# The mixers' output product by Strassen's seven block products, on the machinery of the MLP's down-projection

## The chip, the core and the metric

The kernel runs on one NeuronCore of a Trainium2 chip: TensorE (PE) multiplies matrices into PSUM, VectorE (DVE) and ScalarE (ACT) work elementwise, GpSimd (POOL) masks and loads, SyncE (SP) issues most transfers from HBM. The metric is the device time of one execution in microseconds; of several runs the median is taken.

## The reference, cut to what matters

Two transformer blocks in float32 on 512 tokens of width 1024. The first ends its two mixers (a chunkwise mLSTM, `y_a`, and a stick-breaking attention, `y_b`) with gates and an output product, and goes on with an MLP of width 4096:

```python
gates = jax.nn.sigmoid(jnp.concatenate([g_a, g_b], axis=-1).astype(jnp.float32) + b_gate[l])
y = gates[..., :D_MODEL] * y_a + gates[..., D_MODEL:] * y_b
x = x + y.astype(x.dtype) @ w_out[l]                              # (512 x 1024) @ (1024 x 1024)
h2 = rms_norm(x, norm_mlp_g[l])
x = x + jnp.square(jax.nn.relu(h2 @ w_up[l])) @ w_down[l]
```

The second block (a sparse attention with three branches, gates, an output product and a norm) starts with a norm of this `x`.

## The kernel before

**Products.** Every float32 operand is split into a high part, rounded to fp32r by ScalarE (`split_hi`, L602, for weights), and a fine part, the rest, by VectorE (`split_lo`, L610). A product is three matmuls: high x high, high x fine, fine x high. Weights come in slabs of 1 MB (`slabs`): 1024 rows of 256 columns, or 512 rows of 512 columns ("wide"). A slab is loaded to one of two raw buffers, split into one of two pairs `w_hi`, `w_lo`, and used; a slab's split waits until the slab two before it has been used. Each engine works strictly in the order in which its code is written; semaphores are the only ties between them.

**Gate stage.** Slabs `gb` (4 slabs, 8 tiles of 128 features by 512 tokens, 24 matmuls each, L633) give the second gate. The tiles take turns in the two banks of `ps_g`. For each of them ScalarE applies the sigmoid (L784), VectorE multiplies by `yb_f` (L871) and adds `y_f` (L872), ScalarE casts the sum to `y_hi` (L787), VectorE makes `y_lo` (L875), and only that frees the bank. Before every second tile each of the two engines has a weight split.

**Output product.** Four wide slabs `wo` of `w_out`, 4 token tiles each, 12 matmuls of 128x512 to a tile (`mm_half`, L656). Two tiles go to banks of `ps_z`, two to `ps_g`. VectorE adds each finished tile to `x_sb` (L885).

**Norm and transpose.** `act_rms` squares and sums the four token blocks of x (L944), takes the square root of blocks 0 to 2 and later of block 3 (L948); VectorE takes the reciprocal and scales (`dve_rms`, L958 to L966); TensorE transposes (`feature_tiles`, L684); ScalarE and VectorE write `act_hi`, `act_lo` (L741, L754). This happens ahead of the MLP and again ahead of the second block; the second time its banks become free with the last products (`late`).

**MLP.** Four rounds over quarters of the hidden width. A round has four `up` slabs (8 tiles: relu, square, cast, fine part L880) and then a 512x1024 by 1024x1024 product by Strassen's algorithm in the Winograd form, in seven block products M1, M2, M6, M5, M7, M3, M4, called product 1 to 7 in this order: 256 tokens by 512 by 512, 24 matmuls each (`down_product`, L1277). Its operands need sums of blocks. VectorE makes four sums for each of four feature tiles (`mix_up`, L1890 to L1896) and their fine parts (`mixed_lo`, L1902), and four sums of weight blocks of 128x2048 (`mix_weights`, L1926); ScalarE makes the high parts (L1610). Seven weight splits follow. M1 is copied (L1616), and VectorE adds 14 half products of 128x512 to `x_sb` (L1940). Product 1 needs tiles 0 to 3 of the eight, product 2 tiles 4 to 7.

**Loads.** SP issues all weight loads in one queue: the slabs in order, and the four blocks of `w_down` of a round into `down_raw` (`load_down`), as their buffers come free.

Of the kernel before, what the change touches and what calls it, by code (L numbers as in the profile page):

```python
# [29 lines left out]
P = 128  # L30
# [99 lines left out]
def program(nc, a, out):  # L130

    with ExitStack() as ctx:
# [36 lines left out]
        y_hi = sb("y_hi", [P, KT, S], F32R, at=arena + 3 * K16)  # L169
        y_lo = sb("y_lo", [P, KT, S], F32R, at=arena + 4 * K16)  # L170
# [256 lines left out]
        N_WO = add_wide("wo", a["w_out"], 0, 2)  # L427
        N_MLP = len(slabs)
        for quarter in range(4):
            add("up", a["w_up"], quarter * D, 4)  # L430
            for p in range(PRODUCTS):
                slabs.append((None, quarter, 0, WIDE, "down", p, None))
# [22 lines left out]


# [50 lines left out]
        for n in range(N_ALL):  # L507
            if slabs[n][4] == "down":
                if slabs[n][5] == M7:
                    raw_of[n] = raw_of[n - M7 - 2]  # L510
                    last[raw_of[n]] = n
                continue
# [57 lines left out]
        def raw(n):  # L570

            if slabs[n][4] == "down" and slabs[n][5] != M7:
                return down_raw[DOWN_RAW[slabs[n][5]]]
            return w_raw[raw_of[n]]
# [183 lines left out]
        def act_evacuate(act, n, i):  # L758
# [10 lines left out]
            if kind in ("if", "wo"):  # L769
                return  # L770
# [12 lines left out]
            elif kind == "gb":  # L783
# [3 lines left out]
                nc.scalar.copy(y_hi[:, f, :], ev_t[:, g, :]).then_inc(ev_act, 1)  # L787
# [45 lines left out]
        def dve_evacuate(dve, order, n, i):  # L833
# [175 lines left out]
        def _(sp):  # L1009
# [21 lines left out]
            for n in range(N_MLP):  # L1031
                if n == 1:
                    sp.wait_ge(raw_landed[0], 16)
                load_slab(n)
            down_rows = a["w_down"].rearrange("(q h k p) n -> p q h k n", h=2, k=HALF_K, p=P)

            def load_down(q, i):

                if q == 0:
                    sp.wait_ge(tile_ready, tile_of[N_MLP] - 2)  # L1040
                else:
                    last_split = {0: M6, 1: M4, 2: M5, 3: M3}[i]
                    sp.wait_ge(lo_done, N_MLP + MLP_SLABS * (q - 1) + 4 + last_split + 1)
                    if i == 0:
                        sp.wait_ge(mixed_w, 4 * q)
                src = down_rows[:, q, i % 2, :, WIDE * (i // 2):WIDE * (i // 2 + 1)]
                sp.dma_start(down_raw[i][:], src).then_inc(down_in[i], 16)

            for q in range(4):
                n = N_MLP + MLP_SLABS * q  # L1050
                if q == 0:
                    load_slab(n)
                    load_slab(n + 1)
                    for i in range(4):
                        load_down(q, i)
                else:
                    load_down(q, 0)
                    load_down(q, 2)
                    load_slab(n)
                    load_slab(n + 1)  # L1060
                    load_down(q, 3)
                    load_down(q, 1)
# [24 lines left out]
        def _(pe):  # L1087
# [150 lines left out]
            for n in range(N_WO, N_WO + 4):  # L1238
                mm_slab(pe, n, tile_of[N_GB] if n == N_WO else None, y_hi, y_lo)


            feature_tiles(pe, N_MLP, lambda b: xn[b], lambda b: pe.wait_ge(xn_ready, TB + b + 1),
                          before=N_MLP - 1)
            def down_product(q, p):

                n = N_MLP + MLP_SLABS * q + 4 + p
                up0 = tile_of[n - p - 4]
# [34 lines left out]
            for q in range(4):  # L1282
                n = N_MLP + MLP_SLABS * q
                for j in range(4):
                    mm_slab(pe, n + j, activation_ready=features_ready(pe, N_MLP, 1) if q == j == 0 else None)
                for p in range(PRODUCTS):
                    down_product(q, p)


            def late_banks():  # L1290
                pe.wait_ge(prod_added, added(3, M4, 1))

            pe.wait_ge(prod_added, added(3, M3, 1))
            feature_tiles(pe, N_NQ, lambda b: xn[b], lambda j: pe.wait_ge(xn_ready, 2 * TB + j + 1),
                          late=late_banks)
# [188 lines left out]
        def _(act):  # L1484
# [111 lines left out]
            for n in range(N_GB, N_MLP):  # L1596
                act_slab(act, n)

            act_rms(act, 1, lambda b: wait_tile_free(act, tile_of[N_WO + 3] + b))
            for k in range(KT):  # L1600
                act_feature_tile(act, N_MLP, k, 1, V_MLP)
# [16 lines left out]
            for q in range(4):  # L1618
                n = N_MLP + MLP_SLABS * q
# [23 lines left out]
            act_rms(act, 2, lambda b: act.wait_ge(prod_added, added(3, (M3, M4)[b // 2], b % 2)))  # L1643
# [120 lines left out]
        def _(dve):  # L1764
# [115 lines left out]
            for n in range(N_GB, N_MLP):  # L1880
                dve_slab(dve, order, n)
            dve_rms(dve, order, 1)
            for k in range(KT):
                dve_feature_tile(dve, N_MLP, k, 1, V_MLP)
# [432 lines left out]
```

## Time and profile before

| | us |
|---|---|
| median of 3 runs | 1356.92 |
| lowest, highest | 1356.53, 1358.89 |
| the profiled execution's own time | 1358.28 |
| its span, first to last instruction | 1356.6 |

| engine | busy us | share of the span |
|---|---|---|
| TensorE matmul | 1314.5 | 97% |
| TensorE weight load, beside it | 1098.8 | 81% |
| VectorE | 763.5 | 56% |
| ScalarE | 679.5 | 50% |
| GpSimd | 201.7 | 15% |

The busy share of TensorE is that of pipelined matmuls, whose ends are modelled: a matmul of 512 columns is listed with 0.39 us, but the next one starts earlier. Distances are therefore taken from start to start. The shares of the other engines are averages over stages that differ much, and only rows of the stage itself tell who waits for whom there. A timeline row gives, behind "idle", how long the engine stood still before it and which instruction released it.

### The profile page before, as it was taken

How to read it: one execution, taken by the hardware profiler on the slowest of the kernel's cores; microseconds unless marked ns; L12 is line 12 of the kernel's file. 1: busy time of each engine (PE TensorE's matmuls, PEld its weight loads, DVE VectorE, ACT ScalarE, POOL GpSimd, SP SyncE). 2: the span in 40 equal slices, each digit the busy share in tenths (PEclk: the TensorE clock that was granted, in tenths of full speed). 3: DMA queues.
4: the chain of work that ended last, by engine and by line, in shares of the span. 5: the costliest groups of instructions: out<-in, count | busy, mean ns of one | idle time of the engine just before them, and what ended most of it. 6: DMA issues, size and time to landing. Idle time of an engine off the chain costs nothing.

```text
span 1356.6 us, 17827 instructions
## 1 busy us (share of the span) xinstructions
PE 1314.5 (97%) x7149; PEld 1098.8 (81%) x7149; DVE 763.5 (56%) x1217; ACT 679.5 (50%) x1053; POOL 201.7 (15%) x265
## 2 busy tenths in 40 slices
PE   6999999999999999999999999899999999999998
PEld 4887777787788887878878787788899998989876
DVE  4753444434544544595775858721266767776563
ACT  5244555347666424454635546445245667665232
POOL 1101332261000000000000000003612333331000
PEclk9999999999999999999999999999999999999999
DMA  8657443394435334134070420372612222222311
GB/s 172 103 121 115 73 85 70 88 205 113 62 63 62 81 106 159 59 114 135 1 236 12 154 95 1 93 221 78 139 38 72 71 71 71 69 94 66 108 63 62
DMA packets 94817, 128.97 MB, mean 95 GB/s; under 512 B 5839, under 2 KB 70463, under 8 KB 94736
## 3 DMA queue, kind: packets, MB, share of 16 engines
q1 hardware_dynamic: 88528, 108.70, 31.9%
q0 software_dynamic: 6064, 18.83, 5.3%
q8 instruction: 57, 0.93, 0.3%
q10 hardware_dynamic: 144, 0.31, 0.1%
q14 instruction: 24, 0.20, 0.0%
HBM read 124.94 MB, written 2.88 MB: 94 GB/s over the span
## 4 chain that ended last, share of the span: by engine, by line
PE 86%; DVE 7%; ACT 3%; DMA 2%; issue 2%; SPq 0%; POOL 0%; DVEq 0%; ACTq 0%
PE ps_g L633 44%; PE ps_g L656 8%; PE ps_z L656 8%; PE ps_t L1277 6%; PE ps_z L1388 3%; PE ps_z L1425 2%; PE ps_z L1277 2%; PE ps_t L1460 2%; DVE w_lo L610 2%; DMA w_raw<-in_w_in 2%; PE ps_t L1155 1%; ACT w_hi L602 1%; PE ps_t L1193 1%; PE ps_z L1207 1%; PE ps_t L1310 1%
## 5 line engine op out<-in xcount | busy, mean ns | idle before, releaser
L610 DVE TENSOR_TENSOR w_lo<-w_raw,w_hi 128x2048 fp32r<-128x2048 f32 (+1 forms) x84 | 193.5, 2304 | 233.0 <-ACT w_hi L602 233.0
L633 PE MATMUL ps_g<-act_hi,w_hi 128*128 128x512 f32 x784 | 310.3, 396 | 6.4 <-DVE act_lo L754 4.3
L633 PE MATMUL ps_g<-act_hi,w_lo 128*128 128x512 f32 x784 | 306.7, 391 | 0.0
L633 PE MATMUL ps_g<-act_lo,w_hi 128*128 128x512 f32 x784 | 306.5, 391 | 0.0
L602 ACT ACTIVATE w_hi<-w_raw 128x2048 fp32r<-128x2048 f32 (+1 forms) x84 | 159.2, 1895 | 113.3 <-PE ps_g L656 62.1
L633 PEld LDWEIGHTS ps_g<-act_hi,w_hi 128*128 128x128 f32 x784 | 148.0, 189 | 39.3 <-issue 5.0
L633 PEld LDWEIGHTS ps_g<-act_hi,w_lo 128*128 128x128 f32 x784 | 148.0, 189 | 31.5
L633 PEld LDWEIGHTS ps_g<-act_lo,w_hi 128*128 128x128 f32 x784 | 148.1, 189 | 29.7
L633 PE MATMUL ps_g<-w_hi,act_hi 128*128 128x256 f32 x320 | 93.4, 292 | 0.0
L633 PE MATMUL ps_g<-w_lo,act_hi 128*128 128x256 f32 x320 | 90.3, 282 | 0.0
L633 PE MATMUL ps_g<-w_hi,act_lo 128*128 128x256 f32 x320 | 90.2, 282 | 0.0
L2219 POOL TENSOR_SCALAR cmp_in_k<-pairk,vec 128x124 f32<-128x124 f32 x16 | 11.7, 744 | 503.3 <-ACT pairk L807 503.3
L1697 ACT ACTIVATE probs<-probs,rneg 128x128 f32<-128x128 f32 (+3 forms) x128 | 70.4, 551 | 12.3 <-DVE rneg L2041 10.8
L602 ACT ACTIVATE w_hi<-down_raw 128x2048 fp32r<-128x2048 f32 x24 | 46.0, 1918 | 57.5 <-PE ps_t L1277 35.8
L2239 POOL TENSOR_TENSOR q_parts<-qn,q_parts 64x512 fp32r<-64x512 f32 x32 | 41.9, 1310 | 140.7 <-ACT q_parts L1677 140.5
L633 PEld LDWEIGHTS ps_g<-w_hi,act_hi 128*128 128x128 f32 x320 | 61.1, 191 | 0.2 <-issue 0.2
L633 PEld LDWEIGHTS ps_g<-w_lo,act_hi 128*128 128x128 f32 x320 | 61.2, 191 | 0.0
L610 DVE TENSOR_TENSOR w_lo<-down_raw,w_hi 128x2048 fp32r<-128x2048 f32 x24 | 55.0, 2290 | 10.8 <-ACT w_hi L602 10.8
L633 PEld LDWEIGHTS ps_g<-w_hi,act_lo 128*128 128x128 f32 x320 | 61.0, 191 | 0.0
L2037 DVE CUSTOM_DVE_ANT_0 probs<-ps_z,tile_t 128x128 f32<-128x128 f32 (+3 forms) x128 | 54.9, 485 | 4.5 <-PE ps_z L1388 3.2
L789 ACT ACTIVATE ev_t<-ps_g 128x512 f32<-128x512 f32 x32 | 19.1, 596 | 74.9 <-PE ps_g L633 74.9
L656 PE MATMUL ps_g<-w_hi,act_hi 128*128 128x512 f32 x128 | 49.9, 390 | 0.7 <-DVE act_lo L752 0.7
(349 smaller groups left out, 2602.0 us busy)
## 6 DMA issues: line engine op xcount, KB each, us to landing
w_raw<-in_w_in SPq DMA_DIRECT2D x32, 1024.0 KB, 9.2
w_raw<-in_nsa_w_in SPq DMA_DIRECT2D x22, 1024.0 KB, 5.2
w_raw<-in_w_up SPq DMA_DIRECT2D x16, 1024.0 KB, 5.6
down_raw<-in_w_down SPq DMA_DIRECT2D x16, 1024.0 KB, 5.2
tile_t<-bias_rev_dram POOLq DMA_DIRECT2D x32, 256.0 KB, 3.1
bc<-stat_rows_dram POOLq DMA_DIRECT2D x24, 256.0 KB, 10.2
w_raw<-in_w_out SPq DMA_DIRECT2D x4, 1024.0 KB, 5.0
w_raw<-in_nsa_w_out SPq DMA_DIRECT2D x4, 1024.0 KB, 5.0
```

The lines of the kernel that those rows point to most:

```text
L602: nc.scalar.activation(slab_view(w_hi[b], n), slab_view(raw(n), n), ACT.Copy).then_inc(hi_done, 1)
L610: nc.vector.tensor_tensor(slab_view(w_lo[b], n), slab_view(raw(n), n), slab_view(w_hi[b], n).bitcast(F32), ALU.subtract).then_inc(lo_done, 1)
L633: mm = nc.tensor.matmul(o, stationary, moving, start=(k == 0 and j == 0), stop=(k == KT - 1 and j == 2))
L656: mm = nc.tensor.matmul(bank(t), act[:, k, m], w[:, k - k0, :], start=(k == 0 and j == 0), stop=(k == KT - 1 and j == 2))
L789: nc.scalar.activation(ev_t[:, g, :], ps_g[:, g, :], ACT.Relu).then_inc(ev_act, 1)
L1277: mm = nc.tensor.matmul(down_bank(p, i), act[:, k, m], w[:, k, :], start=(first and k == 0 and j == 0), stop=(k == HALF_K - 1 and j == 2), ...
L1388: mm = nc.tensor.matmul(ps_z[:, at:at + w], q_parts[u % 2][:, b * P:(b + 1) * P], keys[u // 4 % 2][:, 0:w], start=(j == 0), stop=(j == 1))
L1425: mm = nc.tensor.matmul(ps_z[64 * e:64 * e + 64, CAUSAL + at * P:CAUSAL + (at + 1) * P], values[:, s, g * DH:(g + 1) * DH], probs_t[:, blo ...
L1460: mm = nc.tensor.transpose(ps_t[:, at:at + P], probs[u % 2][:, ROWS_AT[b] + s * P:ROWS_AT[b] + (s + 1) * P], ident)
L1697: ins = nc.scalar.activation(p, p, ACT.Exp, bias=rneg[:, u % 2, b:b + 1], accum_out=rsum[:, u % 2, b:b + 1])
L2037: ins = nc.vector.tensor_tensor_reduce(probs[u % 2][:, at:at + w], ps_z[:, at:at + w], tile_t[u % 2][:, S - w:S], 1.0, -3.0e38, ALU.add, A ...
L2239: nc.gpsimd.tensor_tensor(q_parts[u % 2][64 - half:128 - half, :], qn[half:half + 64, 4 * (h // 8) + h % 4, :], q_parts[u % 2][half:half + ...
```

## The change

The output product becomes a round of the MLP's machinery, round 0 of five (`ROUNDS`, `round_at`). Its left operand, the gated sum, is written where the rounds have theirs (`up_raw`, `up_parts`), its weights are the four 512x512 blocks of `w_out`, and the results are added to `x_sb` as in the MLP. The functions of a round (`product_round` on ScalarE and VectorE, `down_product` on TensorE) are called once ahead of the norm, with the `gb` tiles in the place of the `up` tiles, and four times behind it. One block of `w_out` (`b21`) goes to the raw buffer of the last gate slab, because `yb_f` still lies in its usual one. The second weight mix stands ahead of tile 5 in round 0, and ahead of tile 3 in the others. The norm in front of the MLP takes the form of the later one, with its late banks.

```diff
-        N_WO = add_wide("wo", a["w_out"], 0, 2)
+        N_WO = len(slabs)
+        for p in range(PRODUCTS):
+            slabs.append((None, 0, 0, WIDE, "down", p, None))
...
+        ROUNDS = 5
+        def round_at(r):
+            return N_GB if r == 0 else N_MLP + MLP_SLABS * (r - 1)
...
                 after_dve(act, t, 1)
-                nc.scalar.copy(y_hi[:, f, :], ev_t[:, g, :]).then_inc(ev_act, 1)
+                j, k, cols = f // HALF_K, f % HALF_K, slice(0, HALF_S if f < HALF_K else S)
+                nc.scalar.copy(up_parts[j][0][:, k, cols], up_raw[j][:, k, cols]).then_inc(ev_act, 1)
...
                 order.link(nc.vector.tensor_tensor(ev_t[:, g, :], ev_t[:, g, :], yb_f[:, f, :], ALU.mult))
-                nc.vector.tensor_tensor(ev_t[:, g, :], ev_t[:, g, :], y_f[:, f, :], ALU.add)\
+                nc.vector.tensor_tensor(up_raw[j][:, k, :], ev_t[:, g, :], y_f[:, f, :], ALU.add)\
                     .then_inc(ev_dve, 1)
                 after_act(dve, t, 2)
-                nc.vector.tensor_tensor(y_lo[:, f, :], ev_t[:, g, :], y_hi[:, f, :].bitcast(F32),
-                                        ALU.subtract).then_inc(done, 1)
+                nc.vector.tensor_tensor(up_parts[j][1][:, k, cols], up_raw[j][:, k, cols],
+                                        up_parts[j][0][:, k, cols].bitcast(F32), ALU.subtract).then_inc(done, 1)
...
-            elif kind == "wo":
-                tile_done(dve, t)
-                tile_done(dve, t)
-                nc.vector.tensor_tensor(x_sb[:, i, cols], x_sb[:, i, cols], ps, ALU.add)\
-                    .then_inc(done, 1)
...
+                if r == 0:
+                    if i == 0:
+                        for f in (HALF_K - 2, HALF_K - 1):
+                            wait_tile_free(sp, tile_of[N_GB] + f)
+                    elif i == 1:
+                        sp.wait_ge(lo_done, N_WO)
+                        dst = slab_view(raw(N_WO + M2), N_WO + M2)
+                    else:
+                        sp.wait_ge(b_z, HB)
+                    src = out_w[:, i % 2, :, cols]
...
+            for i in (2, 3, 0, 1):
+                load_down(0, i)
...
-            for n in range(N_WO, N_WO + 4):
-                mm_slab(pe, n, tile_of[N_GB] if n == N_WO else None, y_hi, y_lo)
-            feature_tiles(pe, N_MLP, lambda b: xn[b], lambda b: pe.wait_ge(xn_ready, TB + b + 1),
-                          before=N_MLP - 1)
...
+            for p in range(PRODUCTS):
+                down_product(0, p)
+            normed_tiles(0, N_MLP, 1)
...
-            act_rms(act, 1, lambda b: wait_tile_free(act, tile_of[N_WO + 3] + b))
...
+            product_round(0)
+            act_rms(act, 1, lambda b: act.wait_ge(prod_added, added(0, (M3, M4)[b // 2], b % 2)))
...
-                    if f == 3:
+                    if f == (3 if q else 5):
                         mix_weights(q, 1)
```

TensorE's instructions: the 192 matmuls of L656 on `y_hi` and `y_lo` go, 168 more of L1277's kind (now L1286) come, and everything else stays. Three places of the other engines' orders:

VectorE at gated tile 2, the third of the gate stage; `w_lo` is a weight split, `w_raw` on the left a weight mix. Before, then now:

```order
L610 TENSOR_TENSOR w_lo_57<-w_raw_53,w_hi_55 128x2048
L871 TENSOR_TENSOR ev_t<-ev_t,yb_f 128x512
L872 TENSOR_TENSOR ev_t<-ev_t,y_f 128x512
L875 TENSOR_TENSOR y_lo<-ev_t,y_hi 128x512
L871 TENSOR_TENSOR ev_t<-ev_t,yb_f 128x512
```

```order
L619 TENSOR_TENSOR w_lo_57<-w_raw_53,w_hi_55 128x2048
L1940 TENSOR_TENSOR w_raw_53<-down_raw_102,down_raw_101 128x2048
L881 TENSOR_TENSOR ev_t<-ev_t,yb_f 128x512
L883 TENSOR_TENSOR up_raw_97<-ev_t,y_f 128x512
L886 TENSOR_TENSOR up_lo<-up_raw_97,up_hi 128x256
```

A weight mix (L1940, two blocks of `w_out`) has come between the split and the tile.

VectorE from the fine part of gated tile 6 to that of tile 7 (the instruction that writes `y_lo`, now `up_lo` of `up_raw_98`), before with what follows it, then now; `mix` and `up_raw` on the left are block sums of the operand, `down_raw` on the left is a weight mix:

```order
L875 TENSOR_TENSOR y_lo<-ev_t,y_hi 128x512
L871 TENSOR_TENSOR ev_t<-ev_t,yb_f 128x512
L872 TENSOR_TENSOR ev_t<-ev_t,y_f 128x512
L875 TENSOR_TENSOR y_lo<-ev_t,y_hi 128x512
L610 TENSOR_TENSOR w_lo_56<-w_raw_52,w_hi_54 128x2048
L610 TENSOR_TENSOR w_lo_57<-w_raw_53,w_hi_55 128x2048
L885 TENSOR_TENSOR x_sb<-x_sb,ps_z 128x512 x2
```

```order
L886 TENSOR_TENSOR up_lo<-up_raw_98,up_hi 128x512
L1903 TENSOR_TENSOR mix_103<-up_raw_97,up_raw_98 128x256
L1905 TENSOR_TENSOR up_raw_97<-up_raw_97 128x256
L1907 TENSOR_TENSOR up_raw_97<-mix_103,up_raw_97 128x256
L1909 TENSOR_TENSOR up_raw_98<-up_raw_98,up_raw_97 128x256
L1915 TENSOR_TENSOR mix_lo<-up_raw_97,mix_hi 128x256
L1915 TENSOR_TENSOR up_lo<-mix_103,up_hi 128x256
L1940 TENSOR_TENSOR down_raw_99<-w_raw_53,down_raw_99 128x2048
L619 TENSOR_TENSOR w_lo_56<-w_raw_52,w_hi_54 128x2048
L881 TENSOR_TENSOR ev_t<-ev_t,yb_f 128x512
L883 TENSOR_TENSOR up_raw_98<-ev_t,y_f 128x512
L886 TENSOR_TENSOR up_lo<-up_raw_98,up_hi 128x512
```

Four block sums, two fine parts of sums, a weight mix and a weight split have come between the two tiles.

VectorE at the end of the output product, from the last wide slab's split ahead of the last additions to x, to the first step of the norm (`ssq`); before, then now:

```order
L610 TENSOR_TENSOR w_lo_56<-w_raw_52,w_hi_54 128x2048
L610 TENSOR_TENSOR w_lo_57<-w_raw_53,w_hi_55 128x2048
L885 TENSOR_TENSOR x_sb<-x_sb,ps_z 128x512 x2
L885 TENSOR_TENSOR x_sb<-x_sb,ps_g 128x512 x2
L958 TENSOR_SCALAR ssq<-ssq 128x3
```

```order
L619 TENSOR_TENSOR w_lo_57<-down_raw_100,w_hi_55 128x2048
L1954 TENSOR_TENSOR x_sb<-x_sb,ps_t 128x512 x2
L619 TENSOR_TENSOR w_lo_56<-w_raw_53,w_hi_54 128x2048
L1954 TENSOR_TENSOR x_sb<-x_sb,ps_z 128x512
L1954 TENSOR_TENSOR x_sb<-x_sb,ps_t 128x512
L964 TENSOR_SCALAR ssq<-ssq 128x3
```

Before, four additions end the product, one for each token block; now the last two blocks get theirs from the seventh product, behind one more split, and the first two from the sixth.

## Rows read from the trace of the kernel before

**Rows 1.** The page's part 4: share of the last-ending chain by engine.
```profile
PE 86%; DVE 7%; ACT 3%; DMA 2%; issue 2%; SPq 0%; POOL 0%; DVEq 0%; ACTq 0%
```

**Rows 2.** Timeline, TensorE, gate stage to up-projection: start, duration, engine, line, operation, idle.
```profile
464.27 0.39 PE L633 MATMUL ps_g<-act_hi,w_hi 128*128 128x512 f32 x1
...
486.03 0.39 PE L656 MATMUL ps_z<-w_hi,y_hi 128*128 128x512 f32 x1
...
529.32 0.39 PE L656 MATMUL ps_g<-w_hi,y_lo 128*128 128x512 f32 x1
531.88 0.83 PE L684 MATMUL ps_z<-cst,xn 128*128 128x128 f32 x3 [2.16 <-DVE xn L966]
...
538.15 0.47 PE L633 MATMUL ps_g<-act_hi,w_hi 128*128 128x512 f32 x1 [0.89 <-DVE act_lo L754]
```

**Rows 3.** Timeline, TensorE, fourth MLP round's products and the norm behind it.
```profile
847.95 0.51 PE L1277 MATMUL ps_t<-w_hi,up_hi 128*128 128x512 f32 x1 [0.96 <-DVE w_lo L610]
...
869.66 0.39 PE L1277 MATMUL ps_t<-w_hi,up_lo 128*128 128x512 f32 x1
...
878.94 0.47 PE L633 MATMUL ps_g<-act_hi,w_hi 128*128 128x512 f32 x1 [0.89 <-DVE act_lo L754]
```

**Rows 4.** Timeline, VectorE, fourth MLP round, from up tile 7 on.
```profile
834.89 0.68 DVE L880 TENSOR_TENSOR up_lo<-up_raw,up_hi 128x512 fp32r<-128x512 f32 x1
...
837.20 0.42 DVE L1902 TENSOR_TENSOR mix_lo<-up_raw,mix_hi 128x256 fp32r<-128x256 f32 x1
...
838.13 2.29 DVE L610 TENSOR_TENSOR w_lo<-down_raw,w_hi 128x2048 fp32r<-128x2048 f32 x1 [0.17 <-ACT w_hi L602]
840.34 0.42 DVE L1902 TENSOR_TENSOR mix_lo<-up_raw,mix_hi 128x256 fp32r<-128x256 f32 x1
...
843.21 0.68 DVE L1940 TENSOR_TENSOR x_sb<-x_sb,prod 128x512 f32<-128x512 f32 x1
```

**Rows 5.** Timeline, VectorE and ScalarE, gated tiles 0 and 2; last an up tile's cast.
```profile
448.87 0.69 DVE L871 TENSOR_TENSOR ev_t<-ev_t,yb_f 128x512 f32<-128x512 f32 x1 [1.40 <-ACT ev_t L784]
...
450.32 0.62 ACT L787 CAST y_hi<-ev_t 128x512 fp32r<-128x512 f32 x1 [1.49 <-DVE ev_t L872]
...
450.98 0.69 DVE L875 TENSOR_TENSOR y_lo<-ev_t,y_hi 128x512 fp32r<-128x512 f32 x1 [0.69 <-ACT y_hi L787]
...
460.44 0.69 DVE L871 TENSOR_TENSOR ev_t<-ev_t,yb_f 128x512 f32<-128x512 f32 x1
...
545.18 0.41 ACT L794 CAST up_hi<-up_raw 128x256 fp32r<-128x256 f32 x1
```

**Rows 6.** Windows: stretch, length, busy time of PE, PEld, DVE, ACT, POOL, PEclk, DMA, GB/s.
```profile
532.00:535.25 3.25, 3.25 (x16) 3.25 (x17) 2.20 (x5) 0.20 (x1) 0.00 (x0) 0.50 1.05 399
...
848.00:851.25 3.25, 3.25 (x14) 2.67 (x15) 3.25 (x4) 1.00 (x1) 0.00 (x0) 1.00 0.02 5
...
873.50:876.50 3.00, 3.00 (x16) 3.00 (x15) 1.04 (x3) 0.00 (x0) 0.00 (x0) 0.50 0.00 1
```

**Rows 7.** Timeline, ScalarE: a table load amid work, and both norms.
```profile
427.40 1.28 ACT L1583 ACT_TABLE_LOAD   x1
428.70 1.27 ACT L1583 ACTIVATE sp_t<-sp_t 128x1280 f32<-128x1280 f32 x1
...
528.99 1.28 ACT L948 ACT_TABLE_LOAD   x1
530.62 0.20 ACT L948 ACTIVATE rstd<-ssq 128x3 f32<-128x3 f32 x1 [0.35 <-DVE ssq L958]
...
870.54 0.19 ACT L944 ACTIVATION_READ_ACCUMULATOR xn<-x_sb 128x1 f32 x1
870.96 0.20 ACT L948 ACTIVATE rstd<-ssq 128x3 f32<-128x3 f32 x1 [0.23 <-DVE ssq L958]
```

**Rows 8.** The page's part 6: DMA issues, count, KB each, us to landing.
```profile
w_raw<-in_w_out SPq DMA_DIRECT2D x4, 1024.0 KB, 5.0
```

**Rows 9.** Timeline of SP: the gate weights' four issues, start of the first, length.
```profile
391.31 56.56 SPq L1023 DMA_DIRECT2D w_raw<-in_w_in  x4
```

More of the change, by code:

```diff
@@ L431, in program @@
             for p in range(PRODUCTS):
[L432 removed]
+                slabs.append((None, quarter + 1, 0, WIDE, "down", p, None))
         N_NQ = add("nq", NW, NQ, 4)
@@ L511, in program @@
                     last[raw_of[n]] = n
+                elif slabs[n][5] == M2 and slabs[n][1] == 0:
+                    raw_of[n] = raw_of[n - M2 - 1]
+                    last[raw_of[n]] = n
                 continue
@@ L570, in raw @@
         def raw(n):
-            if slabs[n][4] == "down" and slabs[n][5] != M7:
+            if slabs[n][4] == "down" and slabs[n][5] != M7 and n != N_WO + M2:
                 return down_raw[DOWN_RAW[slabs[n][5]]]
@@ L1030, in _ @@
                 sp.dma_start(vec_rows[r0:r0 + k, :], a[name]).then_inc(vec_in, 16)
-            for n in range(N_MLP):
+            for n in range(N_WO):
                 if n == 1:
@@ L1049, in _ @@
[L1049 to L1062, printed above, removed]
+                        sp.wait_ge(mixed_w, 4 * r)
@@ new lines, in load_down @@
+                    src = down_rows[:, r - 1, i % 2, :, cols]
+                sp.dma_start(dst, src).then_inc(down_in[i], 16)
+            for i in (2, 3, 0, 1):
+                load_down(0, i)
+            for r in range(1, ROUNDS):
+                n = round_at(r)
+                load_down(r, 0)
+                load_down(r, 2)
+                load_slab(n)
+                if r == 1:
+                    sp.wait_ge(mixed_w, 4)
+                load_slab(n + 1)
+                load_down(r, 3)
+                load_down(r, 1)
@@ L1280, in down_product, with normed_tiles, late_banks @@
                     mm.then_inc(prod_done, 1)
-            for q in range(4):
-                n = N_MLP + MLP_SLABS * q
+            def normed_tiles(r, n, which):
+                def late_banks():
+                    pe.wait_ge(prod_added, added(r, M4, 1))
+                pe.wait_ge(prod_added, added(r, M3, 1))
+                feature_tiles(pe, n, lambda b: xn[b], lambda j: pe.wait_ge(xn_ready, which * TB + j + 1),
+                              late=late_banks)
+            pe.wait_ge(b_attn, HB)
+            pe.wait_ge(b_out, HB)
+            for p in range(PRODUCTS):
+                down_product(0, p)
+            normed_tiles(0, N_MLP, 1)
+            for r in range(1, ROUNDS):
+                n = round_at(r)
                 for j in range(4):
-                    mm_slab(pe, n + j, activation_ready=features_ready(pe, N_MLP, 1) if q == j == 0 else None)
+                    mm_slab(pe, n + j, activation_ready=features_ready(pe, N_MLP, 1) if r == 1 and j == 0 else None)
                 for p in range(PRODUCTS):
[L1287 to L1295, printed above, removed]
+                    down_product(r, p)
+            normed_tiles(ROUNDS - 1, N_NQ, 2)
             for n in range(N_NQ, N_KS + 1):
@@ L1922, in mix_weights @@
                     dve.wait_ge(lo_done, n + M2 + 1)
-                    out, first, op, second = b21, b21, ALU.subtract, b11
+                    out, first, op, second = b21, b21_raw, ALU.subtract, b11
                 if which:
@@ L1977, in _ @@
                     add_product(q, M4, i)
+            product_round(0)
+            dve_rms(dve, order, 1)
+            for k in range(KT):
+                dve_feature_tile(dve, N_MLP, k, 1, V_MLP)
+            for r in range(1, ROUNDS):
+                product_round(r)
             dve_rms(dve, order, 2)
```

46 lines of the change are left out of this document (19 added, 27 removed).

## The prediction

> **What bounds the kernel now.** I read the chain of work that ended last first: TensorE carries 86% of it and VectorE 7% [rows 1], so a change pays only by taking matmuls off TensorE without making it wait. Then TensorE's own timeline around the product that is rewritten [rows 2]: from 486.03 us, the first of its matmuls, to 529.32 us, the last, there is no wait. There are 192 of them (4 slabs x 4 tiles x 12), so 191 steps take 43.29 us: one starts every 0.2267 us. The next thing TensorE does is wait 2.16 us for the norm and transpose; the first up-projection matmul starts at 538.15 us. Last, the fourth MLP round, which already runs Strassen's seven products and so prices nearly everything that is added [rows 3, 4]. Its products are dense too, but for one wait: the fourth product starts after 0.96 us of idle, released by VectorE's split of its weights [rows 3]. That is the warning here: in that stage VectorE is already as late as TensorE.
>
> **TensorE's own work.** Seven products of 24 matmuls replace 192: 168, so 24 x 0.2267 = **5.44 us less**. The order of TensorE's instructions holds exactly these counts, so that the change doesn't remove this work can be excluded. All that follows is what TensorE waits instead.
>
> **The first new wait: gated tile 4.** Before, a gated tile costs VectorE a multiply, an add, a wait for ScalarE's cast, and the fine part: multiply to fine part 2.11 us (448.87 to 450.98), then 0.69 [rows 5]. Now a weight mix of 128x2048 stands ahead of tile 2's multiply. The nearest row for it is a split of the same shape, 2.21 us from its start to the next instruction (838.13 to 840.34) [rows 4]. Tile 2's multiply was at 460.44 and its weight split starts 0.21 earlier, since the cast ahead of it on ScalarE is half as wide (0.41 instead of 0.62 us) [rows 5]: multiply at 460.44 - 0.21 + 2.21 = 462.44. With the narrower cast, and a fine part of 256 columns (0.42 us, the form at 837.20 [rows 4]), the tile ends 2.11 - 0.21 + 0.42 = 2.32 later, at 464.76. Tile 4 uses the same PSUM bank, and TensorE wanted it at 464.27 [rows 2]. It starts at 464.81: **0.54 us**. A restart after a wait also loses about 0.17: after its wait the fourth product's first matmul to the last of the round takes 869.66 - 847.95 = 21.71 us, where 95 steps of 0.2267 are 21.54 [rows 3].
>
> **The second: product 2.** It needs the fine part of tile 7. In the up rounds that part stands right behind the weight split; here a multiply and an add come first, and VectorE has all the mixing as well. Steps, each start to start: multiply to fine part 2.11 [rows 5]; fine part and four mixing instructions 2.31 (834.89 to 837.20); two fine parts of mixed operands and a weight mix 2.87 (840.34 to 843.21), so 0.66 and 2.21; a weight split 2.21 [rows 4]. Tile 0 ended on TensorE three tiles of 5.44 before 464.27, at 447.95, and its multiply came 0.92 later; so tile 4's multiply is at 464.81 + 0.17 + 5.44 + 0.92 = 471.34. From there VectorE has no gap:
> tile 4: 2.11 + 2.31, then a weight mix 2.21;
> tile 5: 2.11 + 2.31, two fine parts 0.66, a weight split 2.21;
> tile 6: 2.11 + 2.31 + 0.66, a weight mix 2.21, a split 2.21;
> tile 7: 2.11 + 0.69.
> The sum is 26.22: tile 7 is ready at 497.56 us, product 2 starts at 497.61. TensorE is through with tiles 4 to 7 and product 1 at 464.81 + 0.17 + 5 x 5.44 = 492.18. **Wait: 5.4 us, plus 0.17 for the restart.** This alone eats the saving.
>
> **Clock.** After the 2.16 us of idle ahead of the norm, TensorE's granted clock is 0.50 (1.2 of 2.4 GHz) for the whole stretch from 532.00 to 535.25, and it is 0.50 again from 873.50 to 876.50 behind the next norm; after the 0.96 us wait of the fourth product it stays 1.00 [rows 2, 3, 6]. So I expect about 3.3 us at half clock in product 2, which costs 1.65. Bounds: nothing (the wait could end just as the low stretch ends) and twice that.
>
> **The fourth product.** VectorE is still continuous behind tile 7: from that fine part's start to the fourth product's start the last round took 847.95 - 834.89 = 13.06 us [rows 3, 4]. Here: 496.87 + 13.06 = 509.93. TensorE, at half clock in part, has products 2 and 3 done at 497.61 + 0.17 + 10.88 + 1.65 = 510.31. So it now starts on TensorE's time, 510.3; at full clock throughout it would wait until 509.93. From there the later products follow as in the last round, 21.71 us: last matmul at 532.0, against 529.32 before. **Stage: 2.7 us lost**, where TensorE has 5.44 less to do.
>
> **The norm.** Blocks 2 and 3 of x now become final with product 7's two halves, as before the last norm. There the last product matmul to the first of the next projection is 878.94 - 869.66 = 9.28 us [rows 3]; in the rewritten place it was 538.15 - 529.32 = 8.83 [rows 2]. That is 0.45 more. Besides, ScalarE still has the gate's sigmoid table and must load the square root's. Before, the load (528.99, 1.28 us) ended at 530.27, ahead of the square root's release at 530.62: hidden. In the later norm the block's accumulator is read at 870.54 for 0.19 and the square root runs at 870.96, with the table already there [rows 7]. With the load between, 870.73 + 1.30 = 872.03: **1.07 us** of it shows, and the scaling, the transposes and the up-projection wait behind it. The load's length is that of 427.40, whose next instruction starts at 428.70, 1.30 after it [rows 7]. Bounds of the term: 0 (another wait is later) to 1.28.
>
> **What costs nothing.** The four 1 MB loads of w_out take about 5.0 us to land [rows 8]. SP has issued the last gate weights at 447.87 (391.31 + 56.56) [rows 9], two of the four go out right behind, and are there by about 455, for a mix at 460.2. One waits for tile 3's fine part (its tile ends at 464.27, + 0.92 + 2.32 = 467.5) and lands at 472.5, for a mix at 475.8 by the sum above; were it over 3.3 us later, each further us would be a us of product 2. The last goes out behind a split near 471 and is there ten us ahead of its own. SP has nothing urgent queued behind these waits: the first up weights are wanted only in product 7. ScalarE's three more splits (1.9 us each) and its copies lie in its idle time. Six more x additions are inside the 13.06. From the up-projection on nothing changes.
>
> **Sum.** First up matmul at 532.0 + 9.28 + 1.07 = 542.4 instead of 538.15: **+4.2 us**. The profiled execution has a span of 1356.60 and a time of 1358.28, so it would become 1362.5; the median of the three runs is 1.36 lower, 1356.92, and I forecast **1361.1**. A measurement of this kernel can tell about 0.2%, 2.7 us, from no change.
>
> **Rivals.**
> 1. VectorE keeps up. If tile 7 is ready by 492.2, only the short waits stay: -5.44 + 0.71 (tile 4) + 1.13 (fourth product) + 0.45 + 1.07 = -2.1, 1354.8, not slower. It decides at the sum of 26.22: VectorE would have to be 5.4 us shorter between 471.3 and 497.6. For it: VectorE is busy only part of the gate stage before. Against: every piece is from a row, and the order puts them on VectorE one behind the other. 0.08.
> 2. The load of the table is hidden and the clock stays up: 4.2 - 0.4 - 1.07 = +2.7, 1359.6. For it: before, the load was hidden. Against: the earlier block is final later now. 0.10.
> 3. The clock stays low for twice as long after a wait of 5.4 us, longer than any in the middle of this trace: 1.65 more, +5.9, 1362.8. 0.10.
> 4. A table switch also holds ScalarE for a drain of the load's own length, 1.28: +5.5, 1362.4. Row 428.70 speaks against it: work starts 0.02 us after the load. 0.07. (The Trainium skill, "ScalarE: Activation LUTs", section "What ACT_TABLE_LOAD costs", says that a switch costs a load of about 1.28 us and a drain of about 1.38, 2.66 in all; by it the norm's term would be some 1.4 us more than by the rows. The load agrees with this trace, the drain is not seen in it.)
>
> **How the numbers follow.** Forecast 0.60; the rivals 0.35; 0.05 for what I don't see, split evenly between slower and the same. Range: rival 2 with a us of scatter below it (the three runs span 2.4 us), 1358.6, to rival 3 with nearly a us above it, 1363.6; rival 1 and a little are left out. Slower by over 0.2%: forecast, rivals 3 and 4, half of rival 2, which lies on the bound, and half of the unseen, with 0.01 for scatter taken off: 0.83. Faster: rival 1 lies just inside the bound, so half of it, 0.04. The same: 0.13.
>
> **What would show it.** In the new profile: TensorE idle about 5.4 us ahead of the second product, released by the fine part of the last gated tile; VectorE without a gap from tile 4's multiply to that point; about 0.5 us ahead of gated tile 4, released by tile 2; a granted clock of 0.50 behind the long wait; the table load between product 7 and the square root. Wrong would be: a short wait ahead of product 2 (rival 1), or a long one that a DMA releases.

## The result, and the profile after

Time after: **1370.59 us**, median of five runs (1369.65 to 1371.98), against 1356.72 for the kernel before (six runs, 1354.93 to 1360.02). A sixth run of the changed kernel took 2188.41 us at a granted clock of 0.558 and is left out. The ratio is 1.0098, interval 1.0086 to 1.011: about 13 us slower, where 4.2 were forecast. The direction was right; the size lies far outside the range.

The profiled execution took 1369.65 us, with a span of 1367.9 where the kernel before has 1356.6. In the chain of work that ended last, TensorE's share fell from the 86% of [rows 1] to 81%; VectorE's and the DMA's grew:

```profile
PE 81%; DVE 9%; ACT 3%; DMA 3%; issue 2%; POOL 0%; SPq 0%; DVEq 0%; ACTq 0%; POOLq 0%
```

TensorE's timeline (start, duration, then the tile; in brackets the idle time ahead and what ended it) shows the first matmuls of gated tile 4, of product 2, of the norm's transposes and of the up-projection, and ahead of the transposes the last matmul of the last product. They answer to [rows 2]:

```profile
469.67 0.77 PE L642 MATMUL ps_g<-act_hi,w_hi 128*128 128x512 f32 x1 [5.84 <-DVE up_lo L886]
...
504.78 0.76 PE L1286 MATMUL ps_z<-w_hi,up_hi 128*128 128x512 f32 x1 [5.36 <-DVE up_lo L886]
...
539.10 0.39 PE L1286 MATMUL ps_t<-w_hi,up_lo 128*128 128x512 f32 x1
542.82 0.66 PE L693 MATMUL ps_z<-cst,xn 128*128 128x128 f32 x2 [3.34 <-DVE xn L972]
...
549.03 0.47 PE L642 MATMUL ps_g<-act_hi,w_hi 128*128 128x512 f32 x1 [0.89 <-DVE act_lo L763]
```

Product 2 waits 5.36 us, the forecast 5.4. But tile 4, for which 0.54 us were forecast, waits 5.84. VectorE's fine part of tile 2 releases it, so look at what VectorE did before that:

```profile
457.43 2.29 DVE L619 TENSOR_TENSOR w_lo<-w_raw,w_hi 128x2048 fp32r<-128x2048 f32 x1 [1.39 <-ACT w_hi L611]
465.01 2.29 DVE L1940 TENSOR_TENSOR w_raw<-down_raw,down_raw 128x2048 f32<-128x2048 f32 x1 [5.29 <-DMA down_raw<-in_w_out]
```

The first weight mix was due behind the split, at 459.64, and stood until 465.01 waiting for a block of `w_out`; tile 2's evacuation (the steps that empty its PSUM bank), queued behind it on VectorE, stood with it. SP's timeline and the list of loads (number, KB each, median us from issue to landing) say why:

```profile
446.91 0.37 SPq L1029 DMA_DIRECT2D w_raw<-in_w_in  x1
447.32 4.14 SPq L1063 DMA_DIRECT2D down_raw<-in_w_out  x2
```

```profile
w_raw<-in_w_in SPq DMA_DIRECT2D x32, 1024.0 KB, 9.3
down_raw<-in_w_out SPq DMA_DIRECT2D x3, 1024.0 KB, 15.1
```

The two blocks go out 0.4 and 1.3 us behind the last gate slab and take 15.1 and 16.8 us, so they land at 462.4 and 465.0; the third, issued at 472.09, takes 4.9. The last gate slab by itself, in the kernel before and then now:

```profile
w_raw<-in_w_in SPq DMA_DIRECT2D x1, 1024.0 KB, 9.1
```

```profile
w_raw<-in_w_in SPq DMA_DIRECT2D x1, 1024.0 KB, 13.0
```

In stretches of the changed kernel (length, VectorE's busy time, TensorE's granted clock, DMA share, GB/s) the DMA engines are fully busy up to 460, and at first move little:

```profile
448.00:452.00 4.00, 1.81 (x3) 1.00 1.00 103
452.00:456.00 4.00, 1.78 (x3) 1.00 1.04 197
456.00:460.00 4.00, 2.33 (x2) 1.00 0.97 281
460.00:465.00 5.00, 0.00 (x0) 1.00 0.42 162
```

A gate slab takes 9 us by itself, against the 5.0 of a `w_out` load [rows 8]; in the kernel before, with no other load of SP in flight, the engines moved 94 GB/s at a DMA share of 0.87 in the four us from 448 on. Three loads in flight share the engines: they are not three times 5 us side by side, and the last of them landed 18.1 us after the first was issued. (The Trainium skill, "SBUF — State Buffer", section "Can I just issue two DMAs to hit both halves?", says that two concurrent transfers run on the same 16 engines and serialize. This trace agrees in the sum, but not in the order: the slab went out first and still took 13.0 us instead of 9.1.)

### The profile page after: what moved, and what is told of

Same layout as the page of the kernel before. It is cut to its first block, busy times and chain, and to the rows that moved or that the text cites. A ratio compares the mean times of both kernels' runs of the same rounds, so it can differ in the third digit from the quotient of the medians.

```text
span 1367.9 us, 17850 instructions
## 1 busy us (share of the span) xinstructions
PE 1313.7 (96%) x7125; PEld 1097.3 (80%) x7125; DVE 793.2 (58%) x1256; ACT 689.2 (50%) x1068; POOL 202.7 (15%) x265
## 4 chain that ended last, share of the span: by engine, by line
PE 81%; DVE 9%; ACT 3%; DMA 3%; issue 2%; POOL 0%; SPq 0%; DVEq 0%; ACTq 0%; POOLq 0%
PE ps_g L642 42%; PE ps_t L1286 7%; PE ps_g L665 6%; PE ps_z L665 6%; PE ps_z L1286 3%; PE ps_z L1404 3%; DVE w_lo L619 3%; PE ps_z L1441 2%; PE ps_t L1476 2%; ACT w_hi L611 2%; PE ps_t L1169 1%; PE ps_t L1207 1%; DMA down_raw<-in_w_out 1%; PE ps_z L1221 1%; PE ps_t L1326 1%
## 5 line engine op out<-in xcount | busy, mean ns | idle before, releaser
L619 DVE TENSOR_TENSOR w_lo<-w_raw,w_hi 128x2048 fp32r<-128x2048 f32 (+1 forms) x82 | 188.4, 2298 | 216.8 <-ACT w_hi L611 216.8
L611 ACT ACTIVATE w_hi<-w_raw 128x2048 fp32r<-128x2048 f32 (+1 forms) x82 | 155.4, 1895 | 92.9 <-PE ps_g L665 37.8
L611 ACT ACTIVATE w_hi<-down_raw 128x2048 fp32r<-128x2048 f32 x29 | 55.7, 1919 | 69.0 <-PE ps_t L1286 42.8
L619 DVE TENSOR_TENSOR w_lo<-down_raw,w_hi 128x2048 fp32r<-128x2048 f32 x29 | 66.4, 2290 | 12.8 <-ACT w_hi L611 12.8
L1286 PE MATMUL ps_t<-w_hi,up_hi 128*128 128x512 f32 x140 | 54.9, 392 | 3.9 <-DVE w_lo L619 3.9
## 6 DMA issues: line engine op xcount, KB each, us to landing
down_raw<-in_w_out SPq DMA_DIRECT2D x3, 1024.0 KB, 15.1
```

The lines of the kernel that those rows point to most:

```text
L611: nc.scalar.activation(slab_view(w_hi[b], n), slab_view(raw(n), n), ACT.Copy).then_inc(hi_done, 1)
L619: nc.vector.tensor_tensor(slab_view(w_lo[b], n), slab_view(raw(n), n), slab_view(w_hi[b], n).bitcast(F32), ALU.subtract).then_inc(lo_done, 1)
L1286: mm = nc.tensor.matmul(down_bank(p, i), act[:, k, m], w[:, k, :], start=(first and k == 0 and j == 0), stop=(k == HALF_K - 1 and j == 2), ...
```

## The experiments

All edits are to the changed kernel unless it is said otherwise. Theory: the blocks' late landing makes tile 4 wait, and VectorE's backlog makes product 2 wait. Rivals: the backlog alone makes both; the weight mixes are the backlog; the table load or the clock is more than was priced.

**Blocks ahead of the last gate slab** (`e1_early`).

```diff
             for n in range(N_WO):
+                if n == N_WO - 1:
+                    load_down(0, 2)
+                    load_down(0, 3)
                 load_slab(n)
...
-            for i in (2, 3, 0, 1):
+            for i in (0, 1):
```

> The changed kernel, but SP issues the two blocks of w_out that the first weight mix needs ahead of the last gate slab instead of behind it. Theory A (the late landing of these loads holds VectorE ahead of gated tile 2, and so TensorE at gated tile 4): in the trace the mix no longer waits for a DMA, TensorE's wait at tile 4 falls from 5.84 us to the forecast 0.54, its stretch at half clock there (2.3 us of cost) goes too, and the time falls by 7.6 us, from 1370.6 to about 1363.0. The wait ahead of product 2 stays at about 5.4 us, since it comes from VectorE's own chain. Theory B (the chain on VectorE from tile 2 on is simply longer than the sum says, the DMA only happens to land then): the wait at tile 4 stays above 3 us and the time within 2 us of 1370.6.

Measured: 1362.94 us against 1358.04, ratio 1.0039 (1.0024 to 1.0053). The weight mix runs without a wait for a DMA, and TensorE's two waits are:

```profile
459.30 2.29 DVE L1943 TENSOR_TENSOR w_raw<-down_raw,down_raw 128x2048 f32<-128x2048 f32 x1
463.96 0.47 PE L642 MATMUL ps_g<-act_hi,w_hi 128*128 128x512 f32 x1 [0.68 <-DVE up_lo L886]
496.78 0.77 PE L1289 MATMUL ps_z<-w_hi,up_hi 128*128 128x512 f32 x1 [5.35 <-DVE up_lo L886]
```

So the landing, with the half clock behind its wait, is worth nearly 8 us. What is left is +4.9 by the medians and +3.83 at the first up matmul of the traces (93.11 us from tile 0's multiply against 89.28): the forecast's own +4.2 to within the scatter.

**Blocks held back until the slab has landed** (`e6_apart`).

```diff
                     else:
                         sp.wait_ge(b_z, HB)
+                        sp.wait_ge(raw_landed[raw_of[N_WO - 1]], 16 * raw_turn[N_WO - 1])
```

> The changed kernel, but the two blocks of w_out go out only when the last gate slab has landed. Theory A1 (three loads of 1 MB share the DMA engines, of which the gate slab alone takes 9.1 us): the gate slab lands after about 9 us instead of 13.0, the two blocks 5 to 7 us behind it, at about 461 to 463, so the mix starts 2 to 4 us earlier than in the changed kernel and the wait at tile 4 is 2 to 4 us. Theory A2 (the loads of w_out into these buffers are slow in themselves): they take about 15 us again and the wait at tile 4 grows to over 10 us.

Measured, in a single execution: 1369.45 us. The slab lands in 9.0 us, and the two blocks, now sharing only with each other, in 5.3 and 7.5. The list of loads gives the median of all three blocks:

```profile
down_raw<-in_w_out SPq DMA_DIRECT2D x3, 1024.0 KB, 5.3
```

```profile
464.23 2.29 DVE L1941 TENSOR_TENSOR w_raw<-down_raw,down_raw 128x2048 f32<-128x2048 f32 x1 [4.30 <-DMA down_raw<-in_w_out]
468.89 0.77 PE L642 MATMUL ps_g<-act_hi,w_hi 128*128 128x512 f32 x1 [4.84 <-DVE up_lo L886]
```

The blocks are not slow in themselves; they were held up by the slab. Counted from tile 0's multiply the mix comes 1.0 us earlier (15.74 us after it instead of 16.73), and tile 4's wait is 1.0 us shorter. The expectation had 2 to 4: one load behind the other is hardly faster than all at once. What took the wait away was the earlier start in `e1_early`.

**TensorE kept busy ahead of product 2** (`e5_fill`), with the early loads: 22 matmuls whose result nothing reads, called idle matmuls here.

```diff
+                if q == 0 and p == M2:
+                    for j in range(22):
+                        nc.tensor.matmul(ps_t[:, 0:512], act_hi[:, 0, 0:P], act_hi[:, 1, :], start=True,
+                                         stop=True, skip_group_check=True)
                 pe.wait_ge(lo_done, n + 1)
```

> As e1_early, with 22 idle matmuls of 128x512 (5.0 us, result unused) on TensorE between product 1 and product 2, where it waits for VectorE. Theory (half clock follows the long wait): the granted clock stays 1.00 in product 2, its 24 matmuls take 5.4 us instead of about 7.1, but product 4 then waits for VectorE's weight split, so only about 0.4 of the 1.65 us shows in the position of the last product. Rival (the clock falls for another reason, such as the kind of work): the clock is 0.50 there all the same.

Measured, in a single execution: 1361.56 us. In the stretches behind product 2's wait (here TensorE's busy time, its granted clock, DMA share, GB/s) the clock is 0.58 with early loads alone and 1.00 with the idle matmuls:

```profile
497.00:501.00 4.00, 4.00 (x11) 0.58 0.00 0
```

```profile
494.00:498.00 4.00, 3.64 (x17) 1.00 0.00 0
498.00:504.00 6.00, 6.00 (x28) 1.00 0.00 0
```

From tile 4's first matmul to the last product's last it takes 66.45 us instead of 67.03, so 0.6 less: the cost of the half clock, forecast at 1.65 us, is gone, but product 4 now waits for VectorE:

```profile
509.15 0.50 PE L1293 MATMUL ps_t<-w_hi,up_hi 128*128 128x512 f32 x1 [0.85 <-DVE w_lo L619]
```

The clock behind this wait was a small term, and partly covered.

**The square root's table loaded early** (`e2_table`), with the early loads: a square root on one column of constants behind product 5's weight split on ScalarE.

```diff
+                    elif p == M5 and q == 0:
+                        nc.scalar.activation(root_t[:], cst[:, 0:1], ACT.Sqrt)
```

> As e1_early, with one square root of a 128x1 constant on ScalarE between the high parts for products 5 and 6, result unused, so that the table of the square root is loaded there, where ScalarE is idle. Theory (the load shows 1.07 us in the norm): no table load ahead of the norm's square root, the distance from the last product matmul to the first up matmul falls from 9.93 us by 1.0 to 1.1. Rival (the load is covered by another wait): the distance changes by less than 0.3.

Measured, in a single execution: 1360.98 us. The idle ahead of the transposes falls from 3.34 to 2.27 us, as forecast by 1.07:

```profile
534.82 0.41 PE L694 MATMUL ps_z<-cst,xn 128*128 128x128 f32 x2 [2.27 <-DVE xn L973]
```

Yet the last product to the first up matmul takes 9.29 us instead of 9.85, only 0.56 less: from the first transpose to the up matmul it takes 6.63 us instead of 6.12. Both kernels have a stretch at half clock there, at another place: from 535 to 537 with early loads alone, where the transposes begin at 534.72, and from 537 to 539 here, where they begin at 534.82.

**The weight mixes on GpSimd** (`e3_pool`), with the early loads, and **both that and the early table** (`e4_all`). VectorE leaves out the four mixes of this round:

```diff
+            pool.wait_ge(lo_done, n0 - 1)
+            nc.gpsimd.tensor_tensor(t3, b22, b12, ALU.subtract).then_inc(mixed_w, 1)
...
+            nc.gpsimd.tensor_tensor(b21, b21_raw, b11, ALU.subtract).then_inc(mixed_w, 1)
```

> As e1_early, with the four weight mixes of round 0 on GpSimd, which is idle there, instead of VectorE; rounds 1 to 4 keep them on VectorE. Theory (the wait ahead of product 2 is the sum of VectorE's steps from gated tile 4 on): two mixes of 2.21 us leave that sum and one leaves the place ahead of tile 2, so the wait at tile 4 (0.68 us) goes, the wait ahead of product 2 falls from 5.35 us to about 1, the half clock behind it goes, and the first up matmul comes 5 to 6 us earlier than in e1_early: about 1357.5, within 1 us of the kernel before. Rival 1 (GpSimd is slow or holds VectorE up: its tensor operation of 64x512 takes 1.31 us in the trace of the kernel before, so a mix may take 5.2): a mix comes too late for the split of product 3 or product 5, and the wait moves there; the time stays above 1360. Rival 2 (the wait has another cause): the wait ahead of product 2 stays near 5.

> As e3_pool, with the square root's table loaded early as in e2_table. If the theory behind e3_pool holds, another 0.5 us less, about 1357, the same as before or just faster; if the wait ahead of product 2 has moved to another product, no better than e3_pool.

Measured: ratio 1.0105 (1.0088 to 1.0122) and 1.0095 (1.0079 to 1.011), as slow as the change itself. GpSimd's and VectorE's timelines show why:

```profile
461.57 4.87 POOL L2249 TENSOR_TENSOR w_raw<-down_raw,down_raw 128x2048 f32<-128x2048 f32 x1 [27.62 <-DVE w_lo L619]
```

```profile
461.31 0.68 DVE L881 TENSOR_TENSOR ev_t<-ev_t,yb_f 128x512 f32<-128x512 f32 x1
462.03 4.95 DVE L883 TENSOR_TENSOR up_raw<-ev_t,y_f 128x512 f32<-128x512 f32 x1
```

The add on VectorE, 0.69 us elsewhere, lasts 4.95 us, until half a us after the mix on GpSimd has ended. One VectorE instruction beside each of the other three mixes does the same: a fine part of 4.30 us, an add of 4.98 and a block sum of 4.75 (0.69, 0.69 and 0.42 elsewhere). These are the instructions' own durations, not waits ahead of them, so semaphores are not the only tie between the two engines. A mix of 2.2 us on VectorE was replaced by one that holds VectorE for over 4, and the wait ahead of product 2 grew to 6.70 us in `e3_pool` instead of falling. So these two runs do not tell whether the mixes are the backlog.

**The block sums spread over the gate stage** (`e7_spread`), with early loads and early table. The same instructions on VectorE, but the first weight mix stands behind tile 2 instead of ahead of it, and the feature tiles are dealt to the two K halves in turn, so that a block sum is due after every second tile and not only in the second half (`pair_of` gives f % 2 and f // 2 here):

```diff
-                j, k, cols = f // HALF_K, f % HALF_K, slice(0, HALF_S if f < HALF_K else S)
+                j, k = pair_of(n, f)
+                cols = slice(0, S if j else HALF_S)
...
-            out_w = a["w_out"].rearrange("(h k p) n -> p h k n", k=HALF_K, p=P)
+            out_w = a["w_out"].rearrange("(k h p) n -> p h k n", h=2, p=P)
...
+                    elif q == 0 and f % 2:
+                        mix_up(q, f // 2)
```

> The early loads and the early table load are kept, and the feature tiles of the gated output are dealt out to the two K halves of the product alternately (even tiles to the first half, odd ones to the second; the rows of w_out are loaded in the same order). So the block sums of the activations come due after tiles 1, 3, 5 and 7 of the gate stage instead of all after its second half, and the first weight mix is done after tile 2's evacuation. Nothing is left out; VectorE has the same instructions. If VectorE's backlog at the end of the gate stage is what product 2 waits for, most of the 5.35 us before product 2 goes, and the 1.65 us of half clock behind it with it: by VectorE's durations in the traces about 0.8 us are left before product 1, 1.5 before product 2 and 1.0 before product 4, and the granted clock stays at 1.00; the last product's last matmul comes 63.5 us after tile 4's first (67.0 with early loads alone), and tile 4's 0.7 us of wait goes too. With 0.56 for the table load that is 4.9 - 3.5 - 0.7 - 0.6 = 0.1 us over the kernel before: ratio 1.0001, 0.9992 to 1.0012. If product 2 waits for something that does not hang on where the block sums stand (the weights' splits or the blocks' landing), it goes on waiting 5 us and the ratio is 1.003 to 1.004.

Measured: 1355.88 us against 1358.7, ratio **0.9981** (0.9972 to 0.999). TensorE's first matmuls of products 1, 2 and 4 and of the up-projection:

```profile
487.34 0.47 PE L1300 MATMUL ps_z<-w_hi,up_hi 128*128 128x512 f32 x1 [0.56 <-DVE up_lo L890]
494.45 0.47 PE L1300 MATMUL ps_z<-w_hi,up_hi 128*128 128x512 f32 x1 [1.38 <-DVE up_lo L890]
506.42 0.50 PE L1300 MATMUL ps_t<-w_hi,up_hi 128*128 128x512 f32 x1 [0.84 <-DVE w_lo L620]
535.71 0.47 PE L643 MATMUL ps_g<-act_hi,w_hi 128*128 128x512 f32 x1 [0.89 <-DVE act_lo L764]
```

The three waits are 0.56, 1.38 and 0.84 where 0.8, 1.5 and 1.0 were expected, and the clock is 1.00 all through this stage. Tile 4 no longer waits. VectorE's order, with the amount of its work unchanged, was what product 2 waited for. That the kernel is 2.7 us better than expected has a part that nobody planned, and that is luck: the norm's transposes also ran at full clock, and from the first of them to the up-projection it took 4.97 us, where [rows 2] have 6.27. The rest of the 2.7 is not accounted for.

**VectorE's gaps filled** (`e8_gaps`): the low parts of the block sums between a tile's add and its fine part (`meanwhile`), and the fourth mix behind product 4's weight split (the code's M5; the expectation calls it product 5).

```diff
                     .then_inc(ev_dve, 1)
+                meanwhile()
                 after_act(dve, t, 2)
```

> As e7_spread, and the low parts of the block sums are put into the gaps in which VectorE waits for ScalarE's cast of a tile (0.56 to 0.77 us each, tiles 4, 6 and 7), and the fourth weight mix is moved from the start of product 2 to behind product 5's weight split. Nothing is left out; VectorE has the same instructions. By the durations in the traces product 1 and product 4 then wait for nothing and product 2 for 1.8 us; the last product's last matmul comes 62.1 us after tile 4's first, 1.4 us less than in e7_spread: 1.2 us under the kernel before, ratio 0.9991, 0.9980 to 1.0002. If VectorE's idle time in those gaps is not on the path (the rival: ScalarE's casts set the pace of the gate stage's end), it is as e7_spread.

Measured: ratio 0.9977 (0.9968 to 0.9986), no better than `e7_spread` by the intervals. The products did get shorter: counted from tile 0's multiply, the last one's last matmul starts after 77.57 us instead of 78.71. Then the two kernels wait the same 2.27 us, and part. Here are two us of each from about the first transpose on, which starts at 529.29 and 530.74 (columns as for `e5_fill`), first of `e8_gaps`, then of `e7_spread`:

```profile
529.00:530.00 1.00, 0.71 (x4) 0.63 1.05 365
530.00:531.00 1.00, 1.00 (x6) 0.50 0.70 245
```

```profile
531.00:532.00 1.00, 0.83 (x8) 1.00 1.03 367
532.00:533.00 1.00, 1.00 (x11) 1.00 0.11 38
```

The transposes take 6.22 us to the up-projection instead of 4.97, and the gain is given back.

**TensorE kept busy ahead of the norms** (`e9_norm`, on `e8_gaps`), and **the same in the kernel before** (`e10_before`): nine idle matmuls ahead of the wait in the norms before and after the MLP.

```diff
+                for j in range(9):
+                    nc.tensor.matmul(ps_g[:, 0, :], act_hi[:, 0, 0:P], act_hi[:, 1, :], start=True,
+                                     stop=True, skip_group_check=True)
                 pe.wait_ge(prod_added, added(r, M3, 1))
```

> As e8_gaps, with nine matmuls whose result nothing reads (into a bank that the transposes overwrite) ahead of the wait for VectorE's normalised rows in the norms before and after the MLP, to keep TensorE at work through 2.0 of the 2.27 us. Nothing else is changed. In e8_gaps the first norm's transposes to the first up matmul take 6.22 us and the second norm's 6.64 us, partly at half clock; in e7_spread the first norm's took 4.97 us with the granted clock at 1.00. If the idle of 2.27 us is what brings the half clock in, both take about 5.0 us here, 1.2 and 1.6 us less, and the kernel is 3.0 + 2.9 = 5.9 us under the kernel before: ratio 0.9957, 0.9943 to 0.9970. If the transposes themselves bring it in (they keep TensorE less busy than the products), the two stay at 6.2 to 6.6 us and the ratio stays at 0.998.

> The kernel before, with the same nine matmuls ahead of the same two norms and nothing else: how much of e9_norm's gain has nothing to do with the output product. In the kernel before the transposes to the next stage's first matmul take 6.27 us in the norm before the MLP (531.88 to 538.15) and 6.63 us in the one after it. If the idle brings the half clock in, both take about 5.0 us and the ratio is 0.9978 (0.9965 to 0.9990); if the transposes do, 1.0000. Either way e9_norm should stay about 3 us under this kernel, which is what the block algorithm brings once its waits are gone.

Measured: `e9_norm` 1353.2 us, ratio **0.9964** (0.9951 to 0.9976); `e10_before` 1356.85, ratio 0.9993 (0.9984 to 1.0002). The first transposes and the up-projection's first matmul of `e9_norm`:

```profile
530.10 0.41 PE L694 MATMUL ps_z<-cst,xn 128*128 128x128 f32 x2 [0.23 <-DVE xn L978]
535.07 0.47 PE L643 MATMUL ps_g<-act_hi,w_hi 128*128 128x512 f32 x1 [0.89 <-DVE act_lo L764]
```

It is 4.97 us, at a clock of 1.00, and 4.96 in the second norm (869.23 to 874.19), which took 6.64 in `e8_gaps`. With the idle time filled the half clock stays away, so the transposes alone do not bring it; that the same idle time did not bring it in the first norm of `e7_spread` stays unexplained. The kernel before has its two norms shortened alike (to 4.85 and 4.97 us), but gains 1.3 us where 2.9 were expected: two waits for `probs_t` in a later stage, 1.8 us together, are new in its trace. Whether they belong to the edit or to scatter is open. The two kernels lie 3.65 us apart. Of that 2.64 us stand at the first up matmul of their traces (85.21 and 87.85 us from tile 0's multiply), and this much is shown to be the block algorithm's, with most of its own waits gone (1.74 us ahead of product 2 are left).

## Why the prediction was wrong

Compared at the first up matmul, with the traces lined up at tile 0's multiply (448.28 after, 448.87 before): 549.03 + 0.59 - 538.15 = **+11.47 us**, where 4.2 were forecast. Point by point:

1. *TensorE's own work, 5.44 us less.* Right. From product 2 to the last product's last matmul (539.10) it took 34.32 us, forecast 34.39 with its half clock and restarts.
2. *What costs nothing.* **This is the step that failed.** It said that the loads "take about 5.0 us to land" and that the first two "are there by about 455". 5.0 is the time of loads that ran with nothing ahead of them [rows 8]; these ran with the last gate slab, took 15.1 and 16.8 us, and the mix could start only at 465.01 instead of 459.64. The page of the kernel before already gave 9.2 us for a 1 MB slab of `w_in`:

```profile
w_raw<-in_w_in SPq DMA_DIRECT2D x32, 1024.0 KB, 9.2
```

   It was not put into the sum, and that the blocks "go out right behind" was read as a reason for early landing, when it is the reason for a late one.
3. *Gated tile 4.* The wait's mechanism was right as far as it went: without the landing it is 0.68 us (`e1_early`), forecast 0.54. With it, tile 4 starts at 469.67 + 0.59 = 470.26 instead of 464.81: +5.45.
4. *Clock.* The half clock behind product 2's wait was right in place and size: from its first matmul to product 3's first (512.12) it took 7.34 us, 1.73 more than 24 steps and a restart, forecast 1.65. But the wait of 5.84 us, of which the prediction knew nothing, has a half clock of its own (columns as above):

```profile
467.00:475.00 8.00, 5.33 (x14) 0.57 0.17 59
504.00:509.00 5.00, 4.22 (x11) 0.54 0.00 0
```

   From tile 4's first matmul to its multiply on VectorE it took 478.42 - 469.67 = 8.75 us, forecast 6.53: +2.22.

```profile
478.42 0.69 DVE L881 TENSOR_TENSOR ev_t<-ev_t,yb_f 128x512 f32<-128x512 f32 x1 [2.73 <-ACT ev_t L793]
```

5. *Product 2.* The sum of VectorE's chain held almost to the digit: 504.78 - 478.42 = 26.36 us from that multiply, forecast 26.27. The wait ahead of product 2 keeps its forecast size though all came later, since VectorE's chain and TensorE's tiles both start from tile 4.
6. *The fourth product.* Right: it started on TensorE's time, with no wait.
7. *The norm.* Forecast 10.35 us, measured 549.03 - 539.10 = 9.93. The table load shows as forecast, and there is no drain behind it (rival 4):

```profile
540.18 1.28 ACT L954 ACT_TABLE_LOAD   x1
541.48 0.20 ACT L954 ACTIVATE rstd<-ssq 128x3 f32<-128x3 f32 x1
```

   The idle ahead of the transposes is 3.34 us, as forecast; the transposes to the up-projection took 549.03 - 542.82 = 6.21 us, 0.42 less than in the norm that the forecast was taken from.

So 4.2 + 5.45 + 2.22 + 0.09 - 0.07 - 0.42 = 11.47. The landing and the clock that its wait cost are 7.67 us; the small terms take 0.40 back. With the loads moved, the kernel stands where the rest of the prediction put it (ratio 1.0039; 1361.1 against 1356.92 is 1.0031).

Of the rivals, the first, that VectorE keeps up, was false for the order as written but is possible in part: `e7_spread`, 2.8 us under the kernel before, shows that about half of the 5.44 us survives if VectorE's work is spread. The last line of the prediction named "a long one that a DMA releases", ahead of product 2, as what would make it wrong; it came earlier, ahead of gated tile 4, and through VectorE.

The medians stand 13.9 us apart and the profiled executions 11.4 (1369.65 to 1358.28); the difference lies within the scatter of the runs (1354.93 to 1360.02 before).

## What to carry over

Price a load together with what is already in the queue ahead of it and what that takes, not by its own time in an empty queue; and move it ahead of a large neighbour that is not urgent. When an algorithm takes work from the bounding engine and gives it to another, look at when the other's work falls due, not only at its sum: the same instructions made TensorE wait 6.0 us in one order (0.68 and 5.35 in `e1_early`) and 2.8 in another (0.56, 1.38 and 0.84 in `e7_spread`). Time saved ahead of an idle stretch may come back as half clock behind it, so look at the granted clock again after each gain.

## What the runs showed of the hardware

- **GpSimd and VectorE.** A 128x2048 tensor-tensor on GpSimd took 4.58 to 4.99 us, and a two-input instruction that VectorE started beside it lasted until it had ended: 4.95 us instead of 0.69 in `e3_pool`. (The Trainium skill, "SBUF — State Buffer", section "Who interferes with whom", says that a VectorE instruction with two SBUF inputs contends with a GpSimd instruction that reads SBUF. These four places agree.)
- **The slow slab.** A 1 MB gate slab of `w_in` took 9.0 us with the DMA engines to itself (`e6_apart`), 1 MB of `w_out` 5.0 [rows 8]. The slab's shape alone is not the reason: the slabs of `w_up`, also 1024 rows of 256 columns, took 5.6 (median of 16). What the reason is was not tried.
- **The clock.** In the gate stage and the products, idle times of 0.56 to 2.16 us (the longest in `e4_all`) were followed by a granted clock of 1.00, those of 4.84 us (`e6_apart`) and over by one of 0.50. Of two of 2.52 us ahead of tile 4, the one in `e3_pool` was followed by 1.00 and the one in `e4_all` by 0.50. Ahead of the norm's transposes, the same 2.27 us were followed by 0.50 in `e8_gaps` and by 1.00 in `e7_spread` and `e4_all`. What decides in such cases is open.
